# A two-block transformer kernel on one core: the first four weight quarters after a layer norm are multiplied for token tiles 0 to 2 and then for tile 3

## The reference, cut to what matters

```python
for layer in range(2):
    mix = attention(x @ w_in) @ w_out            # layer 0: two kinds of heads, layer 1: "forgetting" attention
    x = layer_norm(ALPHA * x + mix, gain, bias)
    x = layer_norm(ALPHA * x + square(relu(x @ w_up)) @ w_down, gain, bias)   # w_up 1024x4096, w_down 4096x1024
x = second_block(x, c, ...)                       # modulated by columns m = silu(c) @ w_ada + b_ada
```

## Time and profile before

| what | value |
|---|---|
| median of three executions | 2366.84 us |
| lowest and highest of them | 2363.94 and 2367.16 us |
| the profiled execution, its own time | 2362.22 us |
| its span | 2360.5 us |
| its mean granted TensorE clock | 0.925 of 2.4 GHz |
| PE busy | 2119.1 us, 90% of the span |
| DVE, ACT, POOL busy | 1167.5, 731.9 and 440.5 us |
| read from memory | 215.61 MB, 92 GB/s over the span |

### The profile page before, as it was taken

One profiled execution on the slowest core, in us unless ns is written; L12 is line 12 of the kernel. 1 busy time (PEld: TensorE's weight loads), 2 busy tenths in 40 slices (PEclk: granted clock), 3 DMA queues, 4 the chain that ended last, 5 costly groups with the idle time before them and its releaser, 6 DMA issues.

```text
span 2360.5 us, 25614 instructions
## 1 busy us (share of the span) xinstructions
PE 2119.1 (90%) x9416; PEld 1626.8 (69%) x9416; DVE 1167.5 (49%) x2097; ACT 731.9 (31%) x1228; POOL 440.5 (19%) x338
## 2 busy tenths in 40 slices
PE   8977999789999978998889999959999687999996
PEld 6766667668788766875678887845445536888875
DVE  4332345576346343237566256262406654867744
ACT  3210345323223213245243123122213205443441
POOL 2100000000000000039100000000020004767774
PEclk9985789789999998999989999979999897999998
DMA  5231100135335312210235235211110002233333
GB/s 203 90 116 45 27 19 19 54 127 184 116 106 197 107 54 107 96 49 2 108 126 194 89 134 203 109 56 37 72 71 36 18 36 90 107 121 111 125 127 122
DMA packets 39828, 224.91 MB, mean 95 GB/s; under 512 B 5920, under 2 KB 6368, under 8 KB 20144
## 3 DMA queue, kind: packets, MB, share of 16 engines
q1 hardware_dynamic: 27840, 181.17, 21.3%
q0 software_dynamic: 11888, 42.39, 5.7%
HBM read 215.61 MB, written 2.10 MB: 92 GB/s over the span
## 4 chain that ended last, share of the span: by engine, by line
PE 80%; DVE 10%; POOL 5%; ACT 3%; issue 1%; DMA 1%; SPq 0%; POOLq 0%; DVEq 0%; ACTq 0%
PE G L401 33%; PE G L1934 7%; PE TR L1934 4%; PE OB L1934 4%; PE G L905 3%; PE G L1857 3%; PE G L1661 3%; PE OB L1682 2%; POOL SC_sb L682 2%; PE G L1876 2%; PE OB L1004 1%; PE G L1832 1%; DVE stat_sb L2381 1%; PE G L1995 1%; PE G L907 1%
## 5 line engine op out<-in xcount | busy, mean ns | idle before, releaser
L401 PE MATMUL G<-xt_high,weights_high 128*128 128x512 f32 x1128 | 450.0, 399 | 21.1 <-DVE weights_low L424 16.1
L401 PE MATMUL G<-xt_low,weights_high 128*128 128x512 f32 x1128 | 444.0, 394 | 0.0
L401 PE MATMUL G<-xt_high,weights_low 128*128 128x512 f32 x1128 | 443.5, 393 | 0.0
L424 DVE TENSOR_TENSOR weights_low<-ring_sb,weights_high 128x1024 fp32r<-128x1024 f32 x196 | 234.9, 1206 | 385.4 <-ACT weights_high L418 385.3
L418 ACT ACTIVATE weights_high<-ring_sb 128x1024 fp32r<-128x1024 f32 x284 | 293.8, 1044 | 373.8 <-PE OB L1934 136.9
L401 PEld LDWEIGHTS G<-xt_high,weights_high 128*128 128x128 f32 x1128 | 213.8, 190 | 71.4 <-issue 23.4
L401 PEld LDWEIGHTS G<-xt_low,weights_high 128*128 128x128 f32 x1128 | 213.8, 190 | 47.5 <-issue 3.5
L401 PEld LDWEIGHTS G<-xt_high,weights_low 128*128 128x128 f32 x1128 | 213.6, 189 | 46.7 <-issue 1.4
L424 POOL TENSOR_TENSOR weights_low<-ring_sb,weights_high 128x1024 fp32r<-128x1024 f32 x88 | 213.1, 2437 | 74.0 <-ACT weights_high L418 74.0
L1426 DVE SCALAR_TENSOR_TENSOR KS_sb<-G,cols_sb,KS_sb 128x441 f32<-128x441 f32 (+2 forms) x176 | 120.8, 686 | 75.1 <-ACT KS_sb L1182 75.1
L1599 POOL DMA_DIRECT2D KS_sb<-ada x64 | 33.8, 529 | 572.6 <-DVE og_sb L2280 572.6
(11 more groups left out here) (432 smaller groups left out, 3677.4 us busy)
## 6 DMA issues: line engine op xcount, KB each, us to landing
ring_sb<-chunks SPq DMA_DIRECT2D x142, 1024.0 KB, 4.8
KS_sb<-ada POOLq DMA_DIRECT2D x64, 512.0 KB, 4.7
ring_sb<-slabs SPq DMA_DIRECT2D x10, 2048.0 KB, 7.8
qb_sb<-wide_sb SPq DMA_DIRECT2D x24, 128.0 KB, 2.2
X_sb<-x SPq DMA_DIRECT2D x4, 512.0 KB, 6.6
rows_sb<-ln_gain POOLq DMA_DIRECT2D x4, 512.0 KB, 5.3
rows_sb<-ln_bias POOLq DMA_DIRECT2D x4, 512.0 KB, 6.0
out<-X_sb SPq DMA_DIRECT2D x4, 512.0 KB, 4.9
```

Of the source, the lines that this page charges most:

```text
L401: mm = nc.tensor.matmul(out, lhsT=a, rhs=b, start=(3 * i + j == 0), stop=(3 * i + j == n - 1))
L424: tt_(out=Wl[:, n % 4, c], in0=raw_quarter(Q)[:, c], in1=Wh[:, n % 4, c], op=ALU.subtract).then_inc(w_lo, 1)
```

## The change

It has five parts.

1. **Products by token columns.** `first_quarters` takes the place of the quarter-wise start of mlp0, proj1 and mlp1: the first four quarters are multiplied by token columns 0 to 383 (tiles 0 to 2), then by columns 384 to 511 (tile 3). The transposes of tile 3 stand on PE before the first pass of the fourth quarter. A quarter counts as used after its second pass.
2. **Earlier transposes.** PE turns tiles 0 and 1 between the tiles of the stage before (mlp0 to proj1, out1 to mlp1), or right after them (out0 to mlp0), with banks picked by `turn_bank`. ACT's copies and DVE's low parts are put in between the steps of the norm (`norm_to_products`, hooks).
3. **GpSimd splits.** The low parts of quarters 0 and 1 of these three stages move from DVE to POOL.
4. **Down projection.** In the second part of an MLP the last four quarters run tile by tile, in place of two, also where no new start follows (mlp1).
5. **proj1's quarters.** The unused three move from the start of proj1 to its end.

The diff, cut to its core:

```diff
-    FORGET = 4
+    FORGET = 1
-            return slice(0, 8) if stage == "proj1" and 0 < n < FORGET else slice(0, 1024)
+            return slice(0, 8) if stage == "proj1" and n >= 25 else slice(0, 1024)
...
+        def turn_bank(stage, t, h):
+            if stage == "x2":
+                return ((TR[0], G[0]), (TR[1], G[1]), (OB[1], G[2]), (TR[0], TR[1]))[t][h]
+            if stage in ("x1", "x3"):
+                return (TR, OB)[t % 2][h]
+            return TR[h]
...
+        def vector_low(dve, stage, ns):
+            for n in ns:
+                if n == 2:
+                    dve.wait_ge(w_lo, SPLIT0[stage] + 2)
+                low_split(dve, nc.vector.tensor_tensor, stage, n)
+        def gpsimd_low(gp, stage):
+            for n in range(2):
+                low_split(gp, nc.gpsimd.tensor_tensor, stage, n)
...
             gp.wait_ge(gb_in, 32)
+            gpsimd_low(gp, "mlp0")
             gain_bias(1, A["ln_gain"][0, 1, :], A["ln_bias"][0, 1, :])
...
+            gpsimd_low(gp, "proj1")
             fox_gpsimd(gp)
...
             gain_bias(2, A["ln_gain"][1, 0, :], A["ln_bias"][1, 0, :])
+            gpsimd_low(gp, "mlp1")
             ada_loads((2, 3))
...
+            def first_quarters(before, tr_stage, stage, first_tile, outs):
+                for t in range(first_tile, 3):
+                    normalized(before, tr_stage, t)
+                stage_start(stage)
+                pe.wait_ge(tr_out, st(tr_stage, "tr") + 6)
+                for c in (slice(0, 3 * P), slice(3 * P, S)):
+                    for m, o in enumerate(outs):
+                        if c.start == 0 and m == 3:
+                            normalized(before, tr_stage, 3)
+                        if c.start and m == 0:
+                            pe.wait_ge(tr_out, st(tr_stage, "tr") + 8)
+                        pe.wait_ge(w_lo, SPLIT0[stage] + m + 1)
+                        w = [x[:, m, :].rearrange("p (k c) -> p k c", k=KT)[:, :, 0:o.shape[0]] for x in (Wh, Wl)]
+                        mm = split_products(o[:, c], [(w[0][:, k, :], w[1][:, k, :], XTh[:, k, c], XTl[:, k, c]) for k in range(KT)])
+                        if c.start:
+                            mm.then_inc(quarters, 1)
...
-                    with pe.Fori(0, up // 4) as i:
+                    if part == 0:
+                        ada_sums(ada, 0)
+                    with pe.Fori(0 if part else 1, up // 4) as i:
...
-                    for j in range(down - 2 * part):
+                    for j in range(down - 4 * part):
...
-                                w = [x[:, (Q + down - 2 + half) % 4, :].rearrange("p (k c) -> p k c", k=2) for x in (Wh, Wl)]
-                                for k in range(2):
-                                    n = down - 2 + k
+                                for r, j in ((down - 4, down - 3 - half), (down - 2, down - 2 + half)):
+                                    w = [x[:, (Q + j) % 4, :].rearrange("p (k c) -> p k c", k=2) for x in (Wh, Wl)]
+                                    for k in range(2):
+                                        n = r + k
...
-            split_out("out0", turned)
-            transposes("x1", X, lambda t: pe.wait_ge(ln_dve, LN_PLACE["out0", "bi", t]))
-            mlp_products("mlp0", "x1", ada=0)
-            pe.wait_ge(dve_out, st("mlp0", "dve") + 12)
-            transposes("x2", X, lambda t: pe.wait_ge(ln_dve, LN_PLACE["mlp0", "bi", t]))
+            split_out("out0", turned, lambda t: None)
+            first_quarters("out0", "x1", "mlp0", 0, G)
+            mlp_products("mlp0", 0, lambda t: normalized("mlp0", "x2", t - 1) if t in (1, 2) else None)
...
+            first_quarters("mlp0", "x2", "proj1", 2, [G[0][0:16, :]] + G[1:])
+            for g in range(3, 16):
...
+            split_out("out1", mixed, lambda t: normalized("out1", "x3", t - 1) if t in (1, 2) else None)
+            first_quarters("out1", "x3", "mlp1", 2, G)
+            mlp_products("mlp1", 2, lambda t: None)
...
+            def norm_to_products(before, tr_stage, stage, early):
+                root = normalize(before, deferred=True)
+                root(0)
+                root(1)
+                if early:
+                    split_copy(tr_stage, 0)
+                root(2)
+                if early:
+                    split_copy(tr_stage, 1)
+                else:
+                    split_copy(tr_stage, 0)
+                act.wait_ge(quarters, st(stage, "quarters"))
+                high_split(act, stage, 0, first=True)
+                if not early:
+                    split_copy(tr_stage, 1)
+                high_split(act, stage, 1, first=True)
+                split_copy(tr_stage, 2)
+                root(3)
+                for n in (2, 3):
+                    high_split(act, stage, n, first=True)
+                split_copy(tr_stage, 3)
...
+            def between(stage, done, early):
+                if early:
+                    return {("ga", t): (lambda t=t: xt_low_tile(stage, done, t - 1)) for t in (1, 2, 3)}
+                return {("s0", 3): lambda: (xt_low_tile(stage, done, 0), xt_low_tile(stage, done, 1)),
+                        ("ga", 3): lambda: xt_low_tile(stage, done, 2)}
...
-            out_norm("out0")
-            xt_low("x1", 16)
-            mlp("mlp0", ALPHA, ada=0)
-            xt_low("x2", 24)
-            low_splits("proj1", range(4))
+            out_norm("out0", 0, between("x1", 16, False))
+            vector_low(dve, "mlp0", (2, 3))
+            xt_low_tile("x1", 16, 3)
+            mlp("mlp0", ALPHA, 0, between("x2", 24, True))
+            vector_low(dve, "proj1", (2, 3))
+            xt_low_tile("x2", 24, 3)
```

More of the change, by code:

```diff
@@ L1843, in turned, with token_slab @@
                 return XTh[:, k, :], XTl[:, k, :]
-            def token_slab(stage, n0, banks, ready, width=512, between=None, feat=turned):
+            def token_slab(stage, n0, banks, ready, width=512, between=None, feat=turned, unused=0):
                 for p in range(4):
@@ L2114, in relu, with four @@
                 q, a, h = st(stage, "quarters"), st(stage, "act"), st(stage, "hidden")
-                def four(i):
+                def four(i, first=False):
                     for m in range(4):
-                        high_split(act, stage, n + m + 3, i)
+                        if not first or m:
+                            high_split(act, stage, n + m + 3, i)
                         act.wait_ge(quarters, i * 4 + (q + n + m + 1))
@@ L2230, in _ @@
             out_splits("out1", 2)
-            normalize("out1")
-            split_copies("x3")
-            first_splits("mlp1")
+            norm_to_products("out1", "x3", "mlp1", True)
             relu("mlp1")
@@ L2576, in _ @@
             fox_vector(dve)
-            out_norm("out1", 2)
-            xt_low("x3", 32)
-            mlp("mlp1", ALPHA, ada=2)
+            out_norm("out1", 2, between("x3", 32, True))
+            vector_low(dve, "mlp1", (2, 3))
+            xt_low_tile("x3", 32, 3)
+            mlp("mlp1", ALPHA, 2)
             vector_second(dve, down_wait, layer_norm)
```

139 lines of the change are left out of this document (69 added, 70 removed).

## The result

The changed kernel took 2373.21 us (median of 7 runs, 2371.71 to 2377.18), the kernel before 2366.84 (7 runs, 2363.94 to 2367.57): a ratio of 1.0033, 95% interval 1.0021 to 1.0045. It is **slower by 6.4 us** by the medians, 7.8 by the ratio, where I had forecast 10.1 faster.

A forecast was written before the change was run, and what follows sets the result against it. PE's work plus its waits between norms and next products bound the kernel. Terms 6.2 - 17.9 + 0.9 + 0.5 + 4.7 - 5.4 + 0.9 gave -10.1 us: 2356.7 from 2366.84, range 2346 to 2368.

The forecast's parts named there:

- Out0 to mlp0: S: Between out0 and mlp0: with early transposes and hooks, the first products start at 499.1 us, against 506.68.
- The narrow matmul: Second pass over tile 3 in mlp0, proj1 and mlp1: 0.063 us per 128-column matmul, 1.5 us a quarter.
- second-pass matmuls spaced 0.1 or more: Sign that the forecast is wrong, in the 128-column second passes, where it took 0.063 us per matmul.
- S: Start of the first four quarters' products in mlp0, proj1 or mlp1; from it they were to take 25.0 us.
- The bound above (0.188): Upper bound for a 128-column second-pass matmul: 0.188 us, its weight load's row, if loads were not overlapped.
- The lower clock behind short pauses: End of both MLPs: the 2.7 us stall on quarter 15's low split costs 0.9 us of lower clock, between 0 and 1.9.
- The modulation wait: First round of each MLP: PE waits 10.7 us for DVE's ada steps; mlp0's start +6.2 us, mlp1's +4.7.
- S of mlp1: Between out1 and mlp1: the first products start at 1185.9 us, against 1194.40.
- Mlp0 to proj1: Tile 0's residual at 858.5, S at 884.2 against 897.53, next products at 909.2: -17.9 us, with the clock +0.9.
- Mlp1 to the second block: DVE's first residual and PE's next work come 5.4 us earlier: -5.4 us, with the clock +0.9.
- the weight loads: Rival: weight loads set the second pass at 0.188 us per 128-column product, +7.9 us, 2374.7; 8%.
- more starts at the lower clock: Rival: new short PE waits at MLP ends, before proj1 and in out1 add 9.6 us; net -0.5, 2366.3; 18%.

The follow-up runs named there:

- e1: Changed kernel with each half tile of transposes again waiting only for the copy out of the bank it writes: 2366.87 us, ratio 1.0010.
- e4: Kernel before, with each tile's transposes waiting until both halves of the previous tile are copied out: 2379.41 us, ratio 1.0063.
- e13: As e5, but at each MLP's end PE waits for each of the last four quarters' low splits at its first reader: 2340.94 us, ratio 0.9895.
- e5: Changed kernel with the old bank waits and DVE's eight first-round modulation steps per MLP ahead of that round's hidden steps: 2349.11 us, ratio 0.9935.
- e2: Changed kernel with each MLP's first modulation sums moved on PE from ahead of the second round to behind its second quarter: 2365.53 us, ratio 1.0001.

## Why the prediction was wrong

**The step that failed outright: "Out0 to mlp0: S" began the change at out0.** I read the new function for the transposes as a reordering and gave its wait for both halves no term, though the rows of x0's transposes were there to price it: 0.86 a tile, up to 2.6 a set, two sets on the path. Taken out of the changed kernel, it gives back 5.5 to 6.3 us (e1), and the same wait in the old kernel costs 13.4 (e4). With the old wait back the changed kernel is 0.9 us above the kernel before (2366.87 and 2366.01), so this step accounts for most of the loss, and the terms below for the gain that did not come.

**The narrow matmul.** I drew a line through 280 and 512 columns, as if the columns alone set the price, and read 0.063 off it at 128. It is 0.111 with a full weight block, and 0.060 for the forget quarter's 24, so my own sign of being wrong, "second-pass matmuls spaced 0.1 or more", came. In proj1 the 72 full ones on the path cost 72 x 0.048 = 3.5 us; from S (902.06) to the first product behind the four (931.15) I had 25.0 and the profile has 29.1, the other 0.6 in the first pass. In the MLPs the first quarter alone delays DVE, 24 x 0.048 = 1.2 us. The bound above (0.188) held it. The Trainium skill, "TensorE: Matmul & The Clock Gate", section "Back-to-back issue gap", with its 81 ns for 128 columns, was nearer to it than my line was, and still short of this kernel's 0.111.

**The lower clock behind short pauses.** I took 0.9 at each MLP's end. Tile 0's first 12 matmuls took 4.60 at 868.92 and take 2.72 without the pause: 1.9. A further 1.3 us went at the lower clock at the start of mlp0's second down part (granted clock 0.50 from 797.9 to 803 us), behind a pause of 2.27 that the kernel before has too. So tile 0's residual was at 876.28, where my 858.5 and the measured shift of 14.8 give 873.3.

**The modulation wait: right in mechanism, nearly right in size.** S of mlp0 came at 505.74 with out0 6.7 late, so 499.0 against my 499.1; S of mlp1 at 1185.8 against 1185.9, counted the same way. DVE's steps took 12.5 us from the first hidden step to the last (529.71 to 542.16), where I took 13.7. PE's pause was 5.8 (536.42 to 542.21) where I had 10.7, since the second pass itself took 10.8 and not 6.0. The fifth quarter came 6.1 and 4.7 late where I had 4.4 and 2.9, and with the clock behind it 8.1 and 6.6 against 6.2 and 4.7 (means of the two pairs of profiles).

**Mlp0 to proj1.** The chain from tile 0's residual to S was 25.8 us (876.28 to 902.06) against my 25.7. The gain of 15.2 for this stage shrank to 8.6, by the 4.1 behind S and the 3.0 ahead of tile 0's residual, both above.

**Mlp1 to the second block.** I forecast -2.7 for this stage and the two pairs of profiles show +0.3, with about 1 us of scatter. The rows divide it. From the fifth quarter to DVE's first residual of mlp1 the two kernels take 332.6 and 331.9 us (means of two profiles), 0.7 less where I had 2.7; the clock behind the pause at mlp1's end is 0.9 of that miss, and e13's stage is 2.1 shorter than e5's (1134.45 and 1136.51). From there to the second block's transposes it is 32.3 in both, as forecast. Behind them, in code that the change doesn't touch, the changed kernel's profiles are 1.0 longer (776.3 for 775.4), no more than the two of the kernel before differ (775.9 and 774.8).

The misses are 6.3 (bank wait), 6.6 (to proj1's end), 1.7 and 1.8 (the fifth quarters) and up to 3.0 at the end: 16 to 19, against a forecast that missed by 16.5. The rivals that I named all concerned parts of the change that I had priced; none was the part that I had not. The first of them, the weight loads, had the mechanism of the narrow matmul; "more starts at the lower clock" was the nearest in size, and it alone would not have made the kernel slower. That the parts of the sum come close to the total is in part luck, as the stage to out1 carries 2.8 us of chance.

## What to carry to other kernels

A rewritten helper is a change at every place that calls it: compare its waits with the old ones, one by one, and price the difference at each caller, before the part for which it was written. Where work is reordered so that the first result comes later, everything that hangs on first results is compressed behind it; the cure is not to move the waiting instruction but to fill the idle stretch ahead with the part that needs none of it (e5 against e2). And a wait for several operands ahead of a loop is better taken apart, each at its first reader (e13).

## What the runs showed of the hardware that I had not expected

- At the full granted clock, a matmul of this kernel's split fp32r parts with a 128 x 128 weight block of its own goes out every 0.111 us at 128 columns and every 0.120 at 256, then 0.173 at 384 and 0.227 at 512; with a 128 x 16 block it is 0.060 at 128 columns. With full blocks, below 256 columns narrower is hardly faster, and two passes of 384 and 128 cost 0.284 where one costs 0.227.
- Two profiles of the same kernel gave 158.8 and 161.2 us for one stage (granted clock 0.97 and 0.94), and 165.5 and 160.0 (0.90 and 0.94) in the changed one, while the medians of 7 and 10 runs agreed to 1.4 us or better. In this stage a difference of under 5 us in one pair of profiles says nothing; other stages repeated to 0.1 us (the table above).
